# Passages between the layers of a twelve-layer forward pass: two of the four weight splits to GpSimd, another order on VectorE, first tokens turned inside the projection, epsilon moved

## The reference

```python
x = layer_norm(ALPHA * x + h, ln_mix_g[i], ln_mix_b[i])
x = layer_norm(ALPHA * x + swiglu_ffn(x, ffn_w_in[i], ffn_w_down[i]), ln_ffn_g[i], ln_ffn_b[i])
...
x = x + y
x = x + swiglu(rmsnorm(x, norm_ffn_g[i]), f_w13[i], f_w2[i])
```

## Time and profile before

| | us |
|---|---|
| median of 3 runs (2059.07 to 2062.56) | 2061.05 |
| the profiled execution: its time | 2059.04 |
| the profiled execution: its span | 2057.2 |
| busy: TensorE / VectorE / ScalarE / GpSimd | 1993.2 / 1268.0 / 904.4 / 168.8 |

### The profile page before, as it was taken

The page is one execution under the profiler, slowest core; times in us unless marked ns, Lnnn a source line. Parts: engine busy times, 40 slices in busy tenths (PEclk is TensorE's granted clock), DMA queues, the critical chain, the costliest instruction groups (busy, mean ns, idle before and its releaser), DMA issues.

```text
span 2057.2 us, 32468 instructions
## 1 busy us (share of the span) xinstructions
PE 1993.2 (97%) x12754; PEld 1614.9 (79%) x12754; DVE 1268.0 (62%) x1567; ACT 904.4 (44%) x1250; POOL 168.8 (8%) x190
## 2 busy tenths in 40 slices
PE   7999999999999999999999999999999999999999
PEld 6689688878678879888878678877767888897887
DVE  7785655467665556655756755576985554575553
ACT  4462344434444433444545444434434444444442
POOL 2252100010010010000002011002100000000000
PEclk9999999999999999999999999999999999999999
DMA  8321365555166645565455257553324555555554
GB/s 299 115 68 40 108 208 188 184 170 181 52 210 203 198 155 182 171 210 185 164 195 184 72 164 223 192 186 132 103 72 142 185 185 185 166 169 184 184 174 143
DMA packets 92752, 335.95 MB, mean 163 GB/s; under 512 B 11198, under 2 KB 11332, under 8 KB 92335
## 3 DMA queue, kind: packets, MB, share of 16 engines
q1 hardware_dynamic: 85536, 311.62, 45.8%
q0 software_dynamic: 7120, 22.95, 3.9%
HBM read 332.43 MB, written 1.05 MB: 162 GB/s over the span
## 4 chain that ended last, share of the span: by engine, by line
PE 86%; DVE 8%; POOL 2%; issue 2%; ACT 2%; DMA 0%; DVEq 0%; SPq 0%; ACTq 0%; POOLq 0%
PE acc L360 41%; PE acc L439 21%; PE acc L415 9%; PE acc L911 2%; DVE w_lo L1536 2%; PE aux L832 1%; PE aux L616 1%; PE aux L867 1%; POOL rstd L2342 1%; POOL stat L2345 1%; PE aux L459 1%; DVE token_scratch L1612 1%; PE aux L899 1%; PE aux L888 1%; DVE stat L1594 0%
## 5 line engine op out<-in xcount | busy, mean ns | idle before, releaser
L1536 DVE TENSOR_TENSOR w_lo<-w_raw,w_hi 128x1024 fp32r<-128x1024 f32 x588 | 716.7, 1225 | 582.3 <-ACT w_hi L1158 577.3
L1158 ACT ACTIVATE w_hi<-w_raw 128x1024 fp32r<-128x1024 f32 x588 | 620.2, 1059 | 797.2 <-PE acc L360 466.0
L360 PE MATMUL acc<-w_hi,operand_hi 128*128 128x512 f32 x1344 | 534.6, 398 | 26.5 <-DVE operand_lo L1691 12.1
L360 PE MATMUL acc<-w_hi,operand_lo 128*128 128x512 f32 x1344 | 525.4, 391 | 0.0
L360 PE MATMUL acc<-w_lo,operand_hi 128*128 128x512 f32 x1344 | 524.9, 391 | 0.0
L360 PEld LDWEIGHTS acc<-w_hi,operand_hi 128*128 128x128 f32 x1344 | 252.9, 188 | 88.1 <-DVE operand_lo L1557 15.0
L360 PEld LDWEIGHTS acc<-w_hi,operand_lo 128*128 128x128 f32 x1344 | 252.8, 188 | 53.5
L360 PEld LDWEIGHTS acc<-w_lo,operand_hi 128*128 128x128 f32 x1344 | 253.2, 188 | 50.3 <-issue 0.5
L439 PE MATMUL acc<-w_hi,hidden_hi 128*128 128x512 f32 x528 | 210.1, 398 | 0.0
L439 PE MATMUL acc<-w_hi,hidden_lo 128*128 128x512 f32 x528 | 208.5, 395 | 0.0
L439 PE MATMUL acc<-w_lo,hidden_hi 128*128 128x512 f32 x528 | 208.5, 395 | 0.0
(11 more groups left out here) (471 smaller groups left out, 2101.8 us busy)
## 6 DMA issues: line engine op xcount, KB each, us to landing
w_raw<-in_weights SPq DMA_DIRECT2D x588, 512.0 KB, 3.4
ln_gain<-in_gains POOLq DMA_DIRECT2D x7, 512.0 KB, 5.2
bias_at<-in_rpb POOLq DMA_DIRECT2D x12, 256.0 KB, 5.5
ln_gain<-in_ln_g POOLq DMA_DIRECT2D x4, 512.0 KB, 4.0
ln_bias<-in_ln_b POOLq DMA_DIRECT2D x4, 512.0 KB, 5.5
vec_rw<-in_vec POOLq DMA_DIRECT2D x3, 512.0 KB, 6.2
l_rw<-in_lora SPq DMA_DIRECT2D x1, 1152.0 KB, 10.6
iclr_rw<-in_xT SPq DMA_DIRECT2D x2, 512.0 KB, 4.6
```

The costliest lines, as they stand in the source:

```text
L360: mm = pe.matmul(acc[:, 2 * pair + t, :], (ah, al)[x][:, kt, t * P:(t + 1) * P], W[w][:, s, kk * 512:(kk + 1) * 512], start=(kt == 0 and ( ...
L1158: act.activation(whi[:, s, :], raw[:, s, :], ACT.Copy).then_inc(w_hi[s], 1)
L1536: dve.tensor_tensor(wlo[:, s, :], raw[:, s, :], whi[:, s, :].bitcast(F32), ALU.subtract).then_inc(w_lo[s], 1)
```

## The change

- GpSimd gets `split`: in n = 0, 1, 2 and in the rms passages that lead to an ffn or an attention (n = 4, 5, 6, 8, 10) it does the splits of quarters 1 and 2 of the next layer, behind the root of t = 0 and ahead of the root of t = 1. VectorE does quarters 0 and 3.
- VectorE's order in `residual` is written anew: one split behind the norm of t = 0; `add(1)` between the two halves of `operand_lo` of t = 0; the last split behind the norm of t = 1. In the passages to conv and hyena three splits stand behind both operands.
- Layer norm: VectorE adds epsilon (one 128 x 1 operation more) and GpSimd makes the power alone.
- In n = 4, 5, 8 and 10 the turn of t = 0 stands inside `project`, ahead of its last three matmuls. The turn of t = 1 stands behind quarter 2 everywhere (before: behind quarter 1 in the rms passages, 3 in the others).
- ScalarE from n = 4 on: the rounding of quarter 3 stands ahead of the square of t = 1, not behind it.

```diff
@@ -381,11 +381,12 @@
...
                 pe.matmul(ps(bank), ident[:], ident[:].unsqueeze(1).to_broadcast([P, 4, P]), start=True, stop=True)
-        def first_block(q, src, turn_after, after):
+        def first_block(q, src, after):
             keep_busy({"moba": 5, "near": 3}.get(after, 0))
-            turn(src, 0)
+            if src is X or after == "near":
+                turn(src, 0)
             keep_busy({"rwkv": 3, "ffn": 0 if src is tok else 3, "moba": 3, "near": 1}.get(after, 0))
...
                 for i in range(4):
@@ -396,7 +397,7 @@
...
                         mm.then_inc(w_used[(q + i) % SLOTS], 1)
-                    elif i == turn_after:
+                    elif i == 2:
                         turn(src, 1)
         def block_channels(q, pair, operand_waits=False, after={}):
@@ -420,7 +421,7 @@
...
                     after[i]()
-        def project(q, tiles, hi, lo, before, first=0):
+        def project(q, tiles, hi, lo, before, first=0, near_end=None):
@@ -435,6 +436,8 @@
...
                 for c in range(2):
+                    if near_end and c and (kt, t) == steps[-1]:
+                        near_end()
                     for x, w in PE_PASSES:
...
                                        W[w][:, s, c * 512:(c + 1) * 512],
@@ -444,6 +447,10 @@
...
                 seen.add(kt)
+
+        def turn_normed():
+
+            turn(tok, 0)
         def operand_steps():
@@ -833,7 +840,7 @@
...
                 mm.then_inc(m["hidden_turned"], 1)
-            first_block(q, tok if normed else X, 1 if normed else 3, after)
+            first_block(q, tok if normed else X, after)
             with due.loop((FB - 1) // 2, {m["hidden_ready"]: 2 * TT, m["hidden_lo"]: 2}) as i:
                 for b in range(2):
@@ -844,7 +851,7 @@
...
                                 (16, 0): lambda: more_taps(0, 1, 0, 2), (17, 0): lambda: more_taps(0, 1, 1, 0)})
-            project(q + FB * 4, FK, HH, HL, between, first=1)
+            project(q + FB * 4, FK, HH, HL, between, first=1, near_end=turn_normed if following == "near" else None)
         def attention(q, near):
@@ -924,7 +931,7 @@
...
                 else:
-                    first_block(q, tok if near else X, 1 if near else 3, "ffn")
+                    first_block(q, tok if near else X, "ffn")
                 if j == 3:
...
                     turn_qk(QTOK)
@@ -986,7 +993,7 @@
...
             ready = lambda: pe.wait_ge(m["conv_lo_done"], due(m["conv_lo_done"]))
-            project(q + IN_Q, KT, OH, OL, {(0, 0): ready, (0, 1): ready})
+            project(q + IN_Q, KT, OH, OL, {(0, 0): ready, (0, 1): ready}, near_end=turn_normed)
         def hyena(q):
@@ -1138,7 +1145,7 @@
...
                 turn(HX1, t, backwards=(t == 1))
-            project(q + IN_Q, KT, ah, al, operand_steps())
+            project(q + IN_Q, KT, ah, al, operand_steps(), near_end=turn_normed)
         for n, kind in enumerate(layers):
             {"rwkv": rwkv, "ffn": lambda q: ffn(q, n > LAYER_NORMS, layers[n - 1], (layers[n + 1:] or (None,))[0]), "moba": lambda q: attention(q, False), "near": lambda q: attention(q, True),
@@ -1198,12 +1205,9 @@
...
                 operand(0)
-            if n < LAYER_NORMS:
-                ahead(q - 1, 1)
+            ahead(q - 1, 1)
             if rms:
                 square(1)
-            if n >= LAYER_NORMS:
-                ahead(q - 1, 1)
             if more:
                 operand(1)
@@ -1549,9 +1553,9 @@
...
             dve.wait_ge(m["dve_step"], due(m["dve_step"]))
-        def operand(t):
-
-            for h in range(2):
+        def operand(t, halves=(0, 1)):
+
+            for h in halves:
                 dve.wait_ge(m["hi_ready"], due(m["hi_ready"]))
...
                 dve.tensor_tensor(al[own], aux[:, 2 * t + h, :].rearrange("p (k n) -> p k n", n=P), ah[own].bitcast(F32), ALU.subtract)\
@@ -1593,8 +1597,9 @@
...
                 step(last)
-                dve.bn_aggr(mom[:, t, :], stat[:, 32:44]).then_inc(m["ms_ready"], 1)
-                dve.wait_ge(m["ms_ready"], due(m["ms_ready"]))
+                step(dve.bn_aggr(mom[:, t, :], stat[:, 32:44]))
+                dve.tensor_scalar(stat[:, 44 + t:45 + t], mom[:, t, 1:2], LN_EPS, None, ALU.add).then_inc(m["ms_ready"], 1)
+                due(m["ms_ready"])
             def centred(t):
@@ -1632,40 +1637,40 @@
...
                 operand(0)
-                ahead(q - 3, 1)
                 operand(1)
-                ahead(q - 2, 2)
+                ahead(q - 3, 3)
             elif layer_norm:
...
                 normed(0)
-                ahead(q - 4, 2)
+                ahead(q - 4, 1)
+                operand(0, (0,))
+                add(1)
+                operand(0, (1,))
+                moments(1)
+                centred(1)
+                normed(1)
+                ahead(q - 1, 1)
+                operand(1)
+            elif channels:
+                rms_normed(0)
+                ahead(q - 4, 1)
                 add(1)
                 operand(0)
-                moments(1)
-                ahead(q - 2, 1)
-                centred(1)
+                rms_normed(1)
+                operand(1)
+                ahead(q - 3, 3)
+            elif more:
+                rms_normed(0)
+                ahead(q - 4, 1)
+                operand(0, (0,))
+                add(1)
+                operand(0, (1,))
+                rms_normed(1)
                 ahead(q - 1, 1)
-                normed(1)
                 operand(1)
             else:
-                if rms:
-                    rms_normed(0)
-                ahead(q - 4, 1)
                 add(1)
-                if more:
-                    operand(0)
-                ahead(q - 3, 1)
-                if rms:
-                    rms_normed(1)
-                ahead(q - 2, 1)
-                if channels:
-                    operand(1)
-                    ahead(q - 1, 1)
-                else:
-                    ahead(q - 1, 1)
-                    if more:
-                        operand(1)
         def rwkv(q):
             def differences(h):
@@ -2341,10 +2346,24 @@
...
             pool.tensor_tensor(rstd[:, 0:n], stat[:, 0:n], half[:, 0:n], ALU.pow).then_inc(m["rstd_ready"], 1)
-        def power(t, mean_square, scale, eps):
-            pool.tensor_scalar(stat[:, t:t + 1], mean_square, scale, eps, ALU.mult, ALU.add).then_inc(m["eps_added"], 1)
+        def root(t, of):
+            pool.tensor_tensor(rstd[:, t:t + 1], of, half[:, 0:1], ALU.pow).then_inc(m["rstd_ready"], 1)
+
+        def layer_root(t):
+            pool.wait_ge(m["ms_ready"], due(m["ms_ready"]))
+            root(t, stat[:, 44 + t:45 + t])
+
+        def rms_root(t):
+            pool.wait_ge(m["square_ready"], due(m["square_ready"]))
+            pool.tensor_scalar(stat[:, t:t + 1], stat[:, 56 + t:57 + t], 1.0 / D, RMS_EPS, ALU.mult, ALU.add).then_inc(m["eps_added"], 1)
             pool.wait_ge(m["eps_added"], due(m["eps_added"]))
-            pool.tensor_tensor(rstd[:, t:t + 1], stat[:, t:t + 1], half[:, 0:1], ALU.pow).then_inc(m["rstd_ready"], 1)
+            root(t, stat[:, t:t + 1])
+
+        def split(q):
+
+            s = q % SLOTS
+            pool.wait_ge(w_hi[s], nth(q))
+            pool.tensor_tensor(wlo[:, s, :], raw[:, s, :], whi[:, s, :].bitcast(F32), ALU.subtract).then_inc(w_lo[s], 1)
         def load_gain(n):
             load(lng[:], A["ln_g"][n].partition_broadcast(P), m["ln_in"])
@@ -2509,15 +2528,22 @@
         def norms(n):
-            rms = LAYER_NORMS - 1 <= n < len(layers) - 1
-            if n < LAYER_NORMS:
-                for t in range(TT):
-                    pool.wait_ge(m["ms_ready"], due(m["ms_ready"]))
-                    power(t, mom[:, t, 1:2], 1.0, LN_EPS)
-            if rms:
-                for t in range(TT):
-                    pool.wait_ge(m["square_ready"], due(m["square_ready"]))
-                    power(t, stat[:, 56 + t:57 + t], 1.0 / D, RMS_EPS)
+            if n < LAYER_NORMS - 1:
+                layer_root(0)
+                split(start[n + 1] + 1)
+                split(start[n + 1] + 2)
+                layer_root(1)
+            elif n == LAYER_NORMS - 1:
+                layer_root(0)
+                layer_root(1)
+                rms_root(0)
+                rms_root(1)
+            elif n < len(layers) - 1:
+                rms_root(0)
+                if layers[n + 1] not in ("conv", "hyena"):
+                    split(start[n + 1] + 1)
+                    split(start[n + 1] + 2)
+                rms_root(1)
             operands = sum({"rwkv": 8, "hyena": 8, "moba": 4 + PAIRS, "near": 4 + PAIRS}.get(kind, 4) for kind in layers[:n + 1])
```

## The result

| | before | after |
|---|---|---|
| median | 2059.95 (8 runs, 2059.07 to 2063.82) | 2068.97 (8 runs, 2063.69 to 2073.09) |
| profiled execution: time / span | 2059.04 / 2057.2 | 2067.12 / 2065.3 |
| busy TensorE / VectorE / GpSimd | 1993.2 / 1268.0 / 168.8 | 1996.0 / 1274.1 / 204.0 |
| mean granted clock, profiled execution | 0.997 | 0.994 |

The ratio after to before is 1.0040, 95% interval 1.0027 to 1.0053. The loss is 9.0 between these two medians, 8.1 between the profiled spans, and 7.8 against the median of all further executions of the kernel before. The predicted median was 2069.4; the span grew by 8.1 where the sum said 8.35. Over all experiments the kernel before ran in 45 more executions, with a median of 2061.14 and a mean clock of 0.9960. The eight of after have a mean clock of 0.9922.

A forecast was written before the change was run, and what follows sets the result against it. TensorE, busy 97% of the span, was taken to bound the kernel. Layer norm +4.8, n = 3 -1.3, rms passages +2.75 and n = 7 +2.1 gave +8.35 on 2061.05, a median of 2069.4, range 2053 to 2073.

The forecast's parts named there:

- the sum: All passages together: 4.8 - 1.3 + 2.75 + 2.1 = +8.35 on the profiled execution; forecast's chance 0.42.
- Who gets the port in the layer norm passages: n = 0, 1, 2: GpSimd's split starts ahead of VectorE's `normed` and holds it up; +1.6 each.
- rival A: Layer norm passages: VectorE's `normed` gets the port first; -0.55 each instead of +1.6, sum +1.9, 2063.0; chance 0.26.
- +4.8: Layer norm passages n = 0, 1, 2 together, at +1.6 each.
- The power alone: Layer norm: epsilon moves to VectorE; root comes 0.4 behind `centred`'s end, a gain of 0.2 (bounds 0 and 0.3).
- n = 3: Last layer norm, no split on GpSimd: roots 0.2 earlier each, `operand_lo` of t = 1 0.87 earlier; -1.3.
- Rms passages: n = 4, 5, 6, 8, 10: GpSimd's waiting split goes first after `rms_normed`, delaying split 0; +0.55 each, +2.75.
- n = 7: Hyena opening: two more splits ahead of line 2103 make line 816 start 5.1 instead of 3.0 behind first matmul; +2.1.
- B: VectorE keeps the port at a boundary when its next instruction has begun; sum -7.1, 2054.0; chance 0.12.
- C: No exclusion that matters for these sizes, VectorE just has two splits less; sum -13.9, 2047.2; chance 0.12.
- D: GpSimd's split 0.7 or more longer than 2.35, delaying the root of t = 1; 2075 to 2077; chance 0.04.
- n = 9: Three splits behind both operands are ready before quarters 1 to 3 are due; forecast 0.

The follow-up runs named there:

- e1: Changed kernel plus one 128 x 1 memset on GpSimd ahead of its first split in n = 0, 1, 2: median 2069.81.
- e7: Changed kernel plus three tiny 128 x 1 operations on GpSimd ahead of its first split in n = 0, 1, 2: one run, 2060.75.
- e9: Changed kernel plus two idle matmuls ahead of the turn of t = 0 in n = 0, 1, 2 and two behind it in all eight passages: 2069.58.
- e10: e8 with its hyena edit taken back, the f_w_sb line again behind the three splits: median 2048.69.
- e8: Changed kernel with e2's wait, the hyena's f_w_sb line ahead of the splits, and quarter 2's split on VectorE in rms passages: median 2045.93, ratio to before 0.9935.
- e2: Changed kernel with GpSimd's first split waiting for VectorE's split of quarter 0 in all eight passages: median 2054.73, ratio to before 0.9973.
- e5: Changed kernel plus five idle matmuls ahead of the turn of t = 0 in n = 0, 1, 2 and four behind it in all eight passages: 2074.06.

## Why the prediction was right, point by point

**Who gets the port in the layer norm passages (the choice between forecast and rival A).** Right. The forecast rested on the earlier trace rows, a margin of 0.02; here it is 0.13 to 0.16, in all three passages (0.09 in e1). e7 shows how thin it is. Taking 1.93 off for n = 1, forecast and measured: split on GpSimd 431.0 and 430.91, `normed(0)` ends 434.5 and 434.34, split 0 ends 437.9 and 437.63, first matmul 438.55 and 438.29, `normed(1)` 443.55 and 443.29, turn 445.0 and 444.63. The first matmul of t = 1 was put 1.56 later than before; at full clock it is 1.41 later (20.92 against 19.51). In e9, without clock losses, n = 0, 1, 2 are 1.07, 1.25 and 1.28 over before's lengths. For n = 1 this takes 133.33 as before's length at full clock: its 134.72 less 1.39, which is what 1.7 lost there cost in e10 (132.48 against 131.09 in e8, same code). So +4.8 measured 3.6 as a schedule and 5.27 with the clock. The working treated every start as if TensorE ran at full speed behind a gap of 2.6.

**The power alone.** Right in its parts and its sum. The forecast put the root 0.4 behind the end of `centred` and 0.2 earlier than before; it ends 0.42 behind (`centred` ends at 432.44, the power at 432.86), and `normed(0)` starts 4.70 behind add(0), 4.90 before. The row's 1.53 is not the work of a power: it started at 431.33, beside `centred`, and 1.11 of it is waiting for `centred` to end. The 0.56 of the earlier trace rows is a power with no VectorE instruction beside it. In each passage where a power starts beside a VectorE instruction with two SBUF inputs, before and after, it ends 0.4 behind that instruction. So the exclusion holds for a 128 x 1 operation too. The Trainium skill (Perfetto Trace Analysis, "GPSIMD Engine Instruction") calls a GpSimd instruction's span unreliable and says to time by the spacing of starts; 1.53 against 0.56 for the same operation agrees, and here the neighbour's row says what the difference is.

**n = 3.** -1.3 forecast, -1.25 measured.

**Rms passages.** Right as mechanism in all five: the waiter goes first at the boundary, split 0 takes 3.41, the first matmul comes 1.09 late (1.15 forecast), t = 1 at 15.81 behind add(0) where 15.36 was before. +0.55 each measured +0.38 to +0.50, and +1.31 in n = 10 with 1.7 lost to the clock; in e7, whose n = 10 has the code of after and nothing lost, it is +0.29. In all +2.1 as a schedule where +2.75 was said. The root of t = 1 stood clear of the splits by 0.75 (1070.13, behind the ends at 1069.38), as said; e2 shows what it costs when it doesn't.

**n = 7.** The stall forecast at "5.1 instead of 3.0" is 4.99 instead of 3.03. In the one profiled pair 2.0 of it is still there 138 us behind add(0), and 0.46 at its end, behind the slow stretch that only before has there; e10 against e8 gives 2.8 by medians, and the comparison at equal clock loss 0.9 to 1.7. The term of 2.1 is within what these show. The sentence it leaned on, that TensorE's blocks follow each other without a gap between passages, does not hold inside the hyena: in before TensorE stands still there for another 8.8 between 80 and 155 us behind add(0). The waits could have taken the stall up and did not.

**Rivals.** B (VectorE keeps the port at a boundary) and C (no exclusion) are refuted by the lines of n = 5. A did not happen but is what e7 set out to make, and e7 came out better still. D did not happen: the first split of n = 1 in e1 took 2.35, and the two of n = 5 in e2 start 2.36 apart (1051.76 and 1054.12), as in the earlier trace rows.

**What was luck.** That +8.35 and +8.1 lie so near. The port, the boundary and the stall came as forecast, but their sizes came out smaller in that execution: the layer norm term by 1.2 and the rms term by 0.7 as schedules, n = 7 by 1.6, n = 9 by 0.1. The lower clock in n = 0, 1, 2 and 10, of which the sum knew nothing, put 2.7 back, and 0.64 came from ahead of the first passage.

## What to carry to other kernels

Work moved to GpSimd is not beside VectorE's if both read two inputs from SBUF: one of the two waits for the other's whole instruction, and two starts that came first by about 0.1 us on the wrong side cost 3.6 us per layer norm passage. Give the shifted work a semaphore behind the last urgent VectorE instruction, so that it falls beside work on PSUM, and put no more of it ahead of an urgent tiny operation of GpSimd's queue than is done in time: with this wait, one of the two splits of the rms passages back on VectorE, and one line moved, the same idea went from 0.4% slower to 0.65% faster than before. And price each step by what is late next: a dip of the clock or a stall of TensorE counts only where TensorE sets the time.

## What the runs showed of the hardware that I had not expected

- A GpSimd operation of 128 x 1 is held by a running VectorE instruction too: three of them took 1.46 beside `normed(0)` (e7), and one 0.51 instead of 0.19 (e8).
- The power of 128 x 1 took 0.56 with VectorE idle and 1.53 beside `centred`, 1.11 of it waiting. This was there in the kernel before too: its epsilon (1.28 at 429.22) ended with `centred`.
- The granted clock fell behind gaps of TensorE of 2.1 to 2.7 in some passages and not in others that look alike: in the profiled execution of after in n = 0, 2 and 10 (gaps of 2.74, 2.50 and 2.13) and not behind the 2.14 of n = 4 and 5, of e1 in n = 0, 2, 4 and 10. With idle matmuls in the gap these dips were gone (e5, e9), but e9 has two elsewhere.
- Time and mean clock go together within a kernel, 1.2 us for 0.001, but lifting the clock by 0.0026 with idle matmuls gained nothing in the median.
